# State-space layer of a two-layer trunk: input weights turned two pairs at a time, first scan through PSUM, chunks 0 and 1 restacked through memory

## What is computed

```
u = h @ w_in                                     # 256 x 1024, 64 groups of 16 channels
lam_bar = exp(lam * dt)                          # complex, 64 groups x 64 states
b_bar = ((lam_bar - 1) / lam)[..., None] * b_c   # group, state, channel
bu = einsum('bcgh,gph->bcgp', u_chunk, b_bar)
xs = scan over tokens of  x[t] = lam_bar * x[t-1] + bu[t]
y = real(einsum('bcgp,ghp->bcgh', xs, c_c)) + d_skip * u
val, gate = split(gelu(y) @ w_glu);  mix = val * sigmoid(gate)
```

## Time and profile before

| what | value |
|---|---|
| median of 3 runs | 790.54 us (789.68 to 792.15) |
| the profiled execution | 791.36 us, of it 789.6 from the first to the last instruction |
| busy over the span | PE 682.4 (86%), DVE 299.4 (38%), ACT 249.2 (32%), POOL 35.3 (4%) |
| mean granted TensorE clock | 0.954 |
| memory traffic | 237.92 MB, 301 GB/s over the span |
| chain that ended last, share by engine | PE 55%, SP's queue 15%, DMA 12%, DVE 10%, ACT 5% |
| sixteen product records of inputs(c), start to start | 3.45 us |
| state-space layer up to the end of the GLU's first three tiles | 0 to 140 us of the span |

### The profile page before, as it was taken

The page is one execution under the profiler, slowest core; times in us unless marked ns, Lnnn a source line. Parts: engine busy times, 40 slices in busy tenths (PEclk is TensorE's granted clock), DMA queues, the critical chain, the costliest instruction groups (busy, mean ns, idle before and its releaser), DMA issues.

```text
span 789.6 us, 16128 instructions
## 1 busy us (share of the span) xinstructions
PE 682.4 (86%) x6390; PEld 403.8 (51%) x6404; DVE 299.4 (38%) x776; ACT 249.2 (32%) x579; POOL 35.3 (4%) x36
## 2 busy tenths in 40 slices
PE   4898999989977577576899999898989999985994
PEld 4787654555534244244444444555655655652562
DVE  6899761171111011011232534736334433331334
ACT  6687433261111011011311314534233322321224
POOL 1770000000000000000000000000000000000000
PEclk9999999999998887899999999999999999997998
DMA  9335609879999999999990565048999933999981
GB/s 251 112 134 193 186 8 412 346 299 381 419 421 419 422 420 420 422 420 409 381 382 22 213 220 206 0 172 327 424 419 421 420 163 114 423 419 421 419 336 54
DMA packets 64767, 237.92 MB, mean 301 GB/s; under 512 B 24432, under 2 KB 24640, under 8 KB 40128
## 3 DMA queue, kind: packets, MB, share of 16 engines
q1 hardware_dynamic: 63808, 236.82, 75.8%
q10 hardware_dynamic: 896, 0.24, 0.1%
HBM read 235.21 MB, written 1.84 MB: 300 GB/s over the span
## 4 chain that ended last, share of the span: by engine, by line
PE 55%; SPq 15%; DMA 12%; DVE 10%; ACT 5%; issue 2%; DVEq 0%; ACTq 0%
SPq L437 12%; PE ps L1901 12%; PE ps L1992 10%; PE ps L1956 6%; PE ps L1816 6%; PE ps L1881 5%; DMA hT<-in_moe_w_up 4%; DMA ring<-in_moe_w_up 4%; PE ps L1921 4%; DMA ring<-in_moe_w_down 3%; SPq L435 2%; PE ps L2055 2%; PE ps L2066 2%; ACT work L730 2%; PE ps L1964 1%
## 5 line engine op out<-in xcount | busy, mean ns | idle before, releaser
L1901 PE MATMUL ps<-ring,work 128*32 128x256 f32 x1504 | 125.7, 418 | 35.8 <-DMA ring<-in_moe_w_up 12.6
L1901 PEld LDWEIGHTS ps<-ring,work 128*32 128x32 f32 x1504 | 70.6, 120 | 77.9 <-issue 57.6
L1901 PE MATMUL ps<-work 128*32 128x256 f32 x864 | 90.4, 412 | 18.6 <-DMA ring<-in_moe_w_up 6.1
L1433 DVE TENSOR_TENSOR work<-ps,work 128x256 f32<-128x256 f32 x21 | 12.9, 614 | 190.9 <-PE ps L1901 190.9
L1956 PE MATMUL ps<-ring,work 128*32 128x512 f32 x464 | 70.7, 611 | 6.5 <-issue 5.8
L1901 PEld LDWEIGHTS ps<-work 128*32 128x32 f32 x864 | 49.2, 119 | 49.7 <-issue 33.0
L1881 PE MATMUL ps<-work,xr 128*128 128x128 bf16 x736 | 66.4, 219 | 0.7 <-DVE work L1342 0.6
L1881 PE MATMUL ps<-work 128*128 128x128 bf16 x368 | 63.9, 219 | 0.0
L1881 PEld LDWEIGHTS ps<-work,xr 128*128 128x128 bf16 x736 | 57.6, 98 | 8.9 <-issue 3.3
L1992 PE MATMUL ps<-ring,hT 128*128 128x512 f32 x128 | 58.1, 608 | 1.8 <-ACT hT L646 1.8
L1816 PE MATMUL ps<-ring,work 128*128 128x512 f32 x128 | 56.2, 595 | 0.9 <-ACT work L730 0.5
(11 more groups left out here) (338 smaller groups left out, 1070.5 us busy)
## 6 DMA issues: line engine op xcount, KB each, us to landing
ring<-in_moe_w_down SPq DMA_DIRECT2D x22, 2048.0 KB, 24.1
ring<-in_moe_w_gate SPq DMA_DIRECT2D x21, 2048.0 KB, 19.6
ring<-in_moe_w_up SPq DMA_DIRECT2D x16, 2048.0 KB, 30.2
work<-in_moe_w_up SPq DMA_DIRECT2D x12, 2048.0 KB, 20.7
work<-in_moe_w_gate SPq DMA_DIRECT2D x9, 2048.0 KB, 28.9
work<-in_moe_w_down SPq DMA_DIRECT2D x8, 2048.0 KB, 23.8
ring<-in_ssm_w_glu SPq DMA_DIRECT2D x4, 2048.0 KB, 9.0
ring<-in_attn_w_qkv SPq DMA_DIRECT2D x4, 2048.0 KB, 27.5
```

The costliest lines, as they stand in the source:

```text
L1901: ins = mm(ps[s, 6 + j // 2, 0:256], xg[:, k, s], pairs[slots[e // 2]][e % 2][:, k, :], start=(k == 0), stop=(k == KD - 1))
```

## The change

- **Pairs across tiles.** A turned tile now holds two pairs, with the other group of each in the same 64 partitions, so that nothing in W1 is written twice: the combine writes 384 elements, a turn has 4 transposes (one PSUM bank for each half), and four W1 tiles have places of their own. For this B is loaded in eight transfers of 64 partitions instead of two, and lambda and log_dt in six small ones instead of three. The powers that the output weights use are put back into the old order by ScalarE (`swap_powers`), also the B blocks, in eight copies instead of four.
- **Moved from DVE to ScalarE:** the first entry of mu, the negated halves, and mu4 (`multipliers`, `keep_mu4`).
- **First scan through PSUM.** For half 0 the product of `advance` goes to PSUM bank 7 and its multipliers come from bank 0. drive(2), which writes bank 0, waits for `local_done`.
- **Chunk 0 through memory** like the others: keep_u(0), restack(0).
- **Order.** taps(0) and taps(1) move ahead of inputs(7), inputs(3) is cut in two around turn_w1(0, 1), own(0) is cut into pieces around other copies, spread_w2(4) and (5) go behind keep_x(3), the signed C copies go later, skips(0) stands ahead of carries(0) and skips(1) inside carries(1), y is cut into y_taps and y_states, and the GLU pieces are placed between them.

The diff, cut to its core (helpers whose body only moves are left out):

```diff
-        W1 = [v[:, 0:2048].rearrange("p (i r j c) -> p i r j c", i=2, r=OCT, j=SB) for v in (first_of, second_of)]
+        W1 = [v.rearrange("p (i t j c) -> p i t j c", i=2, t=4, j=SB)
+              for v in (first_of[:, 0:1024], second_of[:, 0:1024], first_of[:, 0:1024], second_of[:, 1024:2048])]
+        Ps = first_of[:, 1024:1408].rearrange("p (i j r) -> p i j r", i=3, j=4)
...
+        scan_ps = ps[:, 7, :]
+        mu4_flat = pre[:, 12032:12288]
...
-        powers_ps = ps[:, 6, 0:480].rearrange("p (i j r) -> p i j r", i=3, j=5)
+        powers_ps = ps[:, 6, 0:192].rearrange("p (i t j x) -> p i t j x", i=2, t=16, j=3)
+        mu4_ps = ps[:, 0, 0:64].rearrange("p (o i r) -> p o i r", o=2, i=2)
...
-                sp.dma_start(Bn[:, i, :, :], a["ssm_b_" + n][0].rearrange("(r g) p h -> (g p) r h", g=2)).then_inc(s_bc, 16)
+                for h in range(2):
+                    for g in range(2):
+                        sp.dma_start(Bn[64 * h:64 * h + 64, i, :, :].rearrange("p (t x) c -> p t x c", x=2)[:, :, g, :],
+                                     a["ssm_b_" + n][0].rearrange("(t h x) p c -> h x p t c", h=2, x=2)[h, g]).then_inc(s_bc, 16)
...
+            restack(0)
...
-            dma(lam[:, 0, :], a["ssm_lam_re"][0].rearrange("(r g) p -> r (g p)", g=2), s_lam)
-            dma(lam[:, 1, :], a["ssm_lam_im"][0].rearrange("(r g) p -> r (g p)", g=2), s_lam)
-            dma(small[0:32, 0:2], a["ssm_log_dt"][0].rearrange("(r g) -> r g", g=2), s_lam)
+            for g in range(2):
+                at = slice(16 * g, 16 * g + 16)
+                for i, n in enumerate(("re", "im")):
+                    dma(lam[at, i, :].rearrange("t (h p) -> t h p", h=2),
+                        a["ssm_lam_" + n][0].rearrange("(t h x) p -> x t h p", h=2, x=2)[g], s_lam)
+                dma(small[at, 0:2], a["ssm_log_dt"][0].rearrange("(t h x) -> x t h", h=2, x=2)[g], s_lam)
...
+            def swap_powers():
+
+                act.wait_ge(pow_ready, 1)
+                for g in range(2):
+                    for h in range(2):
+                        dst = Ps[64 * g:64 * g + 64, 0:2, :, :].rearrange("p i j (t h) -> p i j t h", h=2)
+                        src = Pw[64 * h:64 * h + 64, 0:2, 1:5, :].rearrange("p i j (t x) -> p i j t x", x=2)
+                        act.copy(dst[:, :, :, :, h], src[:, :, :, :, g]).then_inc(swapped_ready, 1)
+                act.wait_ge(swapped_ready, 4)
+                act.activation(Ps[:, 2, :, :], Ps[:, 1, :, :], ACT.Copy, scale=-1.0).then_inc(swapped_ready, 1)
+                act.copy(mu[:, 0:2, 0, :], Ps[:, 0:2, 3, :]).then_inc(mu_first, 1)
+
+            def multipliers(to, values):
+
+                act.copy(to[:, 0:4:3], spread(values(0), 1, 2))
+                act.copy(to[:, 2], values(1))
+                act.activation(to[:, 1], values(1), ACT.Copy, scale=-1.0).then_inc(mu4_ready, 1)
+
+            def keep_mu4():
+
+                flat = mu4_flat.rearrange("p (n q r) -> p q n r", n=2, q=4)
+                multipliers(flat, lambda i: mu[:, i, 0:SEG:SEG - 1, :])
+                act.activation(mu[:, 2, :, :], mu[:, 1, :, :], ACT.Copy, scale=-1.0).then_inc(mu4_ready, 1)
...
+            act.wait_ge(c_psum, 1)
+            for i in range(2):
+                act.copy(Cc[:, i, :, :].rearrange("p r c -> p (r c)"), ps[:, 4 + i, :]).then_inc(c_ready, 1)
+            swap_powers()
+            keep_u(0)
...
-            stack_by(0, range(6))
             first(0)
             first(1)
-            stack_by(0, range(6, 16))
             keep_w1T(0, 0)
+            spread_w2(0)
+            keep_w1T(0, 1)
             keep_u(1)
-            keep_w1T(0, 1)
             keep_w1T(1, 0)
-            spread_w2(0)
             first(2)
-            spread_w2(1)
+            first(3)
             keep_x(0, (0, 1))
             keep_w1T(1, 1)
+            spread_w2(1)
+            keep_x(1, (0,))
+            act.wait_ge(mu_ready, 1)
+            act.wait_ge(v_in, 3)
+            multipliers(ps[:, 0, 0:64].rearrange("p (q r) -> p q r", q=4), lambda i: mu[:, i, 0, 0:16])
+            keep_x(1, (1,))
+            keep_mu4()
             spread_w2(2)
-            first(3)
-            keep_x(1, (0, 1))
+            signed_c()
+            blocks_b()
             spread_w2(3)
-            act.wait_ge(cleared, 3)
-            for i in range(2):
-                for g in range(2):
-                    h = slice(64 * g, 64 * g + 64)
-                    act.copy(BB[i][h, :, 16 * g:16 * g + 16], Bb[h, i, :, :]).then_inc(block_b, 1)
             keep_u(2)
             keep_w1T(2, 0)
-            spread_w2(4)
             keep_w1T(2, 1)
-            spread_w2(5)
+            own(0, (0, 1))
             keep_u(3)
             keep_w1T(3, 0)
+            keep_w1T(3, 1)
+            own(0, (2,))
             keep_x(2, (0, 1))
-            keep_w1T(3, 1)
-            own(0)
+            own(0, (3,))
             keep_x(3, (0, 1))
+            spread_w2(4)
+            spread_w2(5)
 
             def gelu(o):
...
+                pw = lambda i: spread(powers_ps[:, i, 4 * o:4 * o + 4], 4, 16)
+                bb = lambda i: spread(of(Bb[:, i, OCT * o:OCT * o + OCT, :]), 2, 3)
+                if o == 2:
+                    dve.wait_ge(w1_turned, 2)
                 for i in range(2):
-                    TTo(v3(t1), pw(0), bb(i), ALU.mult)
-                    link(TTo(v3(second_ps), pw(1), bb(1 - i), ALU.mult))
-                    link(TTo(W1[o % 2][:, i, :, 1:4, :].rearrange("p r j (g c) -> p r j g c", g=2), spread(v3(t1), 3, 2),
-                             spread(v3(second_ps), 3, 2), ALU.add if i else ALU.subtract))
+                    TTo(v5(t1), pw(0), bb(i), ALU.mult)
+                    link(TTo(v5(second_ps), pw(1), bb(1 - i), ALU.mult))
+                    link(TTo(W1[o][:, i, :, 1:4, :].rearrange("p t j (x c) -> p t j x c", x=2), v5(t1), v5(second_ps),
+                             ALU.add if i else ALU.subtract))
...
             weights(0)
             weights(1)
-            link(dve.tensor_copy(mu[:, 0:2, 0, :], Pw[:, 0:2, 4, :]))
+            dve.wait_ge(mu_first, 1)
             step_powers(1, 1, 0, 0)
             step_powers(2, 2, 1, 0)
             step_powers(4, 4, 3, 0)
-            link(TS(mu[:, 2, :, :], mu[:, 1, :, :], -1.0, None, ALU.mult))
+            dve.sem_inc(mu_ready, 1)
             weights(2)
             weights(3)
 
-            ends = lambda i: mu[:, i, 0:SEG:SEG - 1, :]
-            dve.tensor_copy(mu4[:, 0, 0], ends(0))
-            dve.tensor_copy(mu4[:, 1, 0], ends(1))
-            dve.tensor_copy(mu4[:, 0, 1], ends(2))
-            link(dve.tensor_copy(mu4[:, 1, 1], ends(0)))
...
+                dve.wait_ge(mu4_ready, 3 if half else 1)
                 for l in range(1, SEG):
                     n = SEG if l < SEG - 1 else SEG - 1
                     dst = X[:, :, l + 1, rs, :] if l < SEG - 1 else X[:, :, 0, rs, 1:SEG]
-                    advance(dst, X[:, :, l, rs, :], mu4[:, :, :, 0, rs], n)
+                    if half == 0:
+                        advance(dst, X[:, :, l, rs, :], mu4_ps, n, scan_ps)
+                    else:
+                        advance(dst, X[:, :, l, rs, :], mu4[:, :, :, 0, rs], n)
+                if half == 0:
+                    dve.sem_inc(local_done, 1)
...
-            inputs(3)
+            inputs(3, range(4))
             turn_w1(0, 1)
+            inputs(3, range(4, KD))
             turn_w1(1, 0)
             drive(0)
             turn_w1(1, 1)
@@ -1768,31 +1809,36 @@
             inputs(4, range(4, KD))
             inputs(5)
             turn_w1(2, 0)
+            turn_w1(2, 1)
             inputs(6)
-            turn_w1(2, 1)
+            taps(0)
+            taps(1)
             inputs(7)
             turn_w1(3, 0)
+            turn_w1(3, 1)
             drive(2)
-            turn_w1(3, 1)
-            taps(0)
-            taps(1)
             drive(3)
...
-            y(0)
-            y(1)
+            y_taps(0)
+            y_states(0)
+            y_taps(1)
             turn_g(0)
+            y_states(1)
+            glu(0, range(2))
             turn_g(1)
-            glu(0, range(4))
+            glu(0, range(2, 4))
             taps(2)
             taps(3)
             glu(2, range(4))
             pe.wait_ge(f_ready, 32)
-            glu(1, range(4))
-            y(2)
-            y(3)
+            glu(1, range(2))
+            y_taps(2)
+            y_states(2)
+            glu(1, range(2, 4))
             turn_g(2)
+            y_taps(3)
+            y_states(3)
+            glu(0, range(4, 6))
             turn_g(3)
-            glu(0, range(4, KD))
+            glu(0, range(6, KD))
             glu(2, range(4, KD))
             glu(1, range(4, KD))
```

(34 more changed lines are left out.)

121 lines of the change are left out of this document (49 added, 72 removed).

## The result

| | before | after |
|---|---|---|
| median of 20 runs each | 791.60 us (788.45 to 795.66) | 795.76 us (790.49 to 798.60) |
| the profiled execution, its span | 791.36, 789.6 | 790.53, 788.7 |
| mean granted TensorE clock, profiled execution | 0.954 | 0.950 |

The changed kernel is slower: ratio 1.0051, 95% interval 1.0034 to 1.0068, about 4 us. I had forecast 786.7 with a range up to 790.4. I therefore read a second one as well, `same_again`, the same kernel once more: 796.33 us, span 794.5.

What follows compares the result with a forecast made beforehand. Bound taken: VectorE to the first scan, ScalarE, then TensorE's GLU products to 140 us. GLU end -5.7, clock +1.9: -3.8, 791.36 to 787.6, or 786.7 in the median's frame; own range 785.6 to 788.5, overall 784.0 to 790.4.

Steps and rivals of the forecast that it cites:

- step 5: TensorE's clock: one fall at the wait before drive(3), costing 1.9 us in drive(3) and y; bounds 0 and 3.8.
- Step 1: VectorE up to the first scan: 7.6 us less work, scan able to start at 46.6 or 46.7 instead of 54.35.
- Step 2: First scan's input: drive(0) at 34.8, drive(1) at 41.8, ready just under 46.6, so the scan starts then.
- Step 3: First scan to y: scan ends at 58.1, drive(3) starts at 68.8, GLU begins at 80.0 instead of 87.61.
- Step 4: GLU stage: 50.9 us of work plus 3.4 of waits from 80.0, ending at 134.3, 5.7 earlier.
- low clock still there after 76: Sign on TensorE's clock, listed among those that would show the forecast wrong.
- Rival D: Clock falls at the wait for chunk 3, stays low until about 85: +5.3 us, 795.8; chance 0.07.
- The start: Three more parameter DMA issues (about 0.45 each) before ScalarE's first table load: cost 0, above 0.6 us.
- lambda 0 to 1: Unknown cost at the kernel's beginning: lambda loaded in six parts, 0 to 1 us.
- Rival C: B's eight loads arrive late, 4 us later at 25, shifting the front 3.7: 790.4, no change; chance 0.15.
- E: The change doesn't reach the end (earlier weight-stream limit or order mistake): within 1 of 790.5; chance 0.10.
- B: TensorE's clock stays up, no wait as long as 3.83 being left: -5.7 us, 784.8; chance 0.20.

Runs made afterwards that it cites:

- warm_all: Changed kernel plus eight unread filler products in TensorE's waits ahead of the parameter turns, drive(1), drive(2) and drive(3); 788.98 us, ratio 0.9965.
- chunk0_stacked: Changed kernel with chunk 0 stacked by ScalarE again (16 copies) instead of going through memory; 793.48 us, ratio 1.0029.
- before_b8: Kernel before the change, with B loaded in eight transfers to 64 partitions instead of two to 128; 791.89 us, ratio 0.9998.
- warm_lam_sp: Changed kernel with all waits filled and the second half of the lambda and log_dt loads issued by SP; 788.17 us, ratio 0.9966.
- before_kept_warm: Kernel before the change, with four filler products in its one wait ahead of y(0); 791.59 us, ratio 1.0009.
- before_lam6: Kernel before the change, with lambda and log_dt in six loads on ScalarE's queue instead of three; 792.05 us, ratio 1.0002.
- warm_scan_sbuf: Changed kernel with all waits filled and the first scan's products in SBUF instead of PSUM; 793.14 us, ratio 1.0029.

## Why the prediction was wrong, point by point

Forecast were 3.8 us less, measured are 4.2 more (791.60 to 795.76), 8.0 apart. The term that failed is the clock of step 5: priced at 1.9, at most 3.8, it measures 6.2 to 6.8, which is 4.3 to 4.9 of the 8.0. The other 3.1 to 3.7 are sizes: with its clock kept up the changed kernel is 2.6 below before, where the forecast without a fall has 5.7. Some 1.5 of that stands in the profile at the GLU's start.

- **Step 1 (VectorE) held.** Combines 0.55, as priced. The scan started at 47.5, not 46.6, behind the later start. "I price the PSUM form like the SBUF form" was right for the product, 0.69 against 0.692, and the adds stay at 0.42 beside GpSimd. Left in SBUF the scan would have cost 3.6 more, and half the gain of the step would have gone.
- **Step 2 held in its mechanism, late by the start.** drive(0) 36.1 (forecast 34.8), drive(1) 42.9 (41.8). Ahead of drive(1) TensorE waited 0.90, which the step did not name.
- **Step 3 held but for sizes.** drive(2) at 64.4, forecast 62.1: chunk 2 was staged at 57.3 instead of 55.65, because ScalarE's moved copies ended 1.7 late, and its way through memory took 0.6 more. TensorE waited 1.67 there. The step's own numbers leave a wait of about 0.8 (inputs(7) done at 60.3, two turns, drive(2) at 62.1), but it is named nowhere, and step 5 did not count it. With the waits filled the GLU starts at 81.5 (forecast 80.0 with no fall).
- **Step 4 held.** From GLU start to end 54.3 in after, `same_again` and `warm_all`, forecast 54.3. The rest of the span is 648.0 to 650.0 in twelve of the fourteen profiles behind that and 652.5 and 652.7 in two, with no trend between the kernels, so a microsecond at 140 does count as one. The scatter I did not take apart.
- **Step 5 failed.** "I take one fall, 1.9 in drive(3) and y. Bounds: no fall, 0, and two falls, 3.8." The changed kernel has one long fall or two or three shorter ones, and the clock is low for up to 17 us on end, where before had 6. The sign that the prediction had set against itself, "low clock still there after 76", stands in after's rows (75 to 82 at 0.50). Filled waits give back 6.2 to 6.8 (795.2 and 795.76 to 788.98) in the changed kernel, and 2.3 (791.6 to 789.32) in the kernel before. I looked for single long waits, and had in the trace only such falls as follow them. I passed over the waits near 1 us ahead of drive(1) and 1.7 ahead of drive(2); the rows of 65 to 82 show that the clock then stays low through 17 us of steady work. The wait for chunk 3 came too, 3.93 in `same_again` and 6.02 in `chunk0_stacked`. Its write to memory took 3.1 and 4.0 us there, against 2.0 in after (SP's issues: 68.04 to 71.17, 67.41 to 71.40, 63.21 to 65.23); and with the taps moved forward TensorE has less work of its own to cover it, which I read from the order of its list and did not test.
- **Rival D**, with a chance of 0.07 and 795.8, has the kind of cause and nearly the number, but the number is luck. D lets one stretch, from the wait for chunk 3 to 85, cost 11 us. `same_again` has just that stretch, and it cost 3.4; the rest of the loss came from the fall at 46 to 54, which D does not have, and from a gain that was smaller than 5.7. Its objection, that before recovered amid short matmuls, was drawn from one execution of another order of work. Where the clock falls varies from one execution to the next, and no single price could have been right.
- **The start** (bound 0 to 0.6, lambda 0 to 1): the first work on x came 1.2 later, twice the upper bound, since the finely cut lambda loads take 0.61 each to issue and not 0.45. Over all profiles the step is larger still: 7.34 to 8.01 in the seven with all six loads on ScalarE, 5.76 to 6.16 in the four of before's order with three. Moving three of them to SP gave 1.5 there; at the end it is worth 0.8 to 1.4 by the medians (788.98 to 788.17, 795.2 to 793.8), inside the intervals; about half of what is won at the start goes into the wait for the last C load. The own range of the forecast was also added up wrongly: -0.9 to +1.5 around 786.7 is 785.8 to 788.2.
- **Rival C** is small: priced at 3.7, nothing in `before_b8`, a wait of 0.69 in after and none in `same_again`, up to 1.10 where the start is early. **E** fell: the front moves the end. **B** is what `warm_all` makes, forecast 784.8, measured 788.98.

At a clock that is kept up on both sides, the forecast of the edit was 5.7 less the 1.9 of before's own fall, 3.8. The profiles give 137.49 less 135.76, 1.7: 1.5 is the late GLU start, and the kernel before begins its GLU at 85.1 there, 0.6 earlier than 87.61 less 1.9. Counted from the start of inputs(0) (14.62 and 16.18), the new order is 3.3 shorter to the end of the GLU tiles, close to the 3.8; the later start takes 1.6 of it back. The medians (789.32 and 788.98) show only 0.3, with overlapping intervals. So the edit by itself is worth 0 to 2 us, and it costs 3.9 to 4.5 of clock (6.2 to 6.8 less the 2.3 of before).

What stays open: which property of the front, the waits, the halved number of transposes or both, brings the fall at 46 to 54, since fillers mend both at once. Idle time ahead of it does not explain it by itself: from 28 to 46 us the old order waits more (14.98 of 18 us busy in before, with waits of 0.73, 1.45 and 0.84) and never falls there, while the new order is busy for 17.1 of 18 in after, which does not fall there, and for 17.0 in `same_again`, which does. Open too is why the falls at 22 to 28 come in some executions of either kernel, and why inputs(0) starts at 15.82 in one execution of the changed kernel and at 17.28 in another, with only 0.4 between their first works on x.

## What to carry to other kernels

An edit that shortens TensorE's work and leaves its waits should be priced at both levels of the clock: list every wait that TensorE has after the change, those of a microsecond included (here falls followed waits of about 1 and of 1.67), and set against the gain what the work behind each would cost at half speed (here up to 17 us of it). Compare the mean granted clock over many executions before believing a profile, because one profile can be the lucky one. Products that nobody reads, in waits that are there anyway, turned this change from 1.0051 to 0.9965; the fastest kernels here, `warm_all` and `warm_lam_sp`, both have them. Try them on the unchanged kernel as well before crediting the edit: it went to 0.9976 by them alone. And one filled wait can give nothing (`before_kept_warm`, 1.0009).

## What the runs showed of the hardware that was not expected

- The clock stayed at 0.50 for 17 us of unbroken TensorE work (65 to 82 in after).
- Two executions of one and the same kernel differ by 4.5 us at the end of the GLU tiles (140.15 and 144.62). Of this 1.5 is there at the start of inputs(0) (15.82 and 17.28); the rest arises where the clock falls in different places.
- Issuing a small load from ScalarE's queue took 0.41 to 0.49 with rows kept whole (one of six 0.79, `before_lam6`) and 0.60 to 0.74 for the same bytes cut finer (after).
- An add of two SBUF operands of 256 columns took 0.49 to 1.37 beside GpSimd's multiplications and 0.42 to 0.43 without them (`warm_scan_sbuf`); with one of the two in PSUM it took 0.42 beside them (after).
